# Attention blocks weighed three steps behind their scores instead of two, with the queues around it reordered

## The reference

```
s = einsum('bqhmd,bkhmd->bhmqk', q, k2) * 64 ** -0.5
s = where(dist >= 0, s + bias, NEG_INF)
p = softmax(s, axis=-1)
a = p[:, :, 0] - lam * p[:, :, 1]
o = einsum('bhqk,bkhd->bqhd', a, v)
o = rmsnorm(o, subln_gain, 1e-5) * (1 - lambda_init)
```

## Time and profile before

| | |
|---|---|
| time, median of 3 runs | 1475.78 us (1474.71 to 1475.9) |
| profiled execution | 1474.49 us, its span 1472.7 us |
| PE busy | 1399.6 us (95%) |
| DVE busy | 718.0 us (49%) |
| ACT busy | 461.9 us (31%) |
| POOL busy | 179.1 us (12%) |
| chain that ended last | PE 89%, DVE 4%, issue 2%, POOL 2%, ACT 1%, DMA 1% |
| from 290 to 511 us | PE busy 193.72 of 221.00 us |

### The profile page before, as it was taken

The page is one execution under the profiler, slowest core; times in us unless marked ns, Lnnn a source line. Parts: engine busy times, 40 slices in busy tenths (PEclk is TensorE's granted clock), DMA queues, the critical chain, the costliest instruction groups (busy, mean ns, idle before and its releaser), DMA issues.

```text
span 1472.7 us, 22577 instructions
## 1 busy us (share of the span) xinstructions
PE 1399.6 (95%) x8834; PEld 1259.0 (85%) x8834; DVE 718.0 (49%) x1066; ACT 461.9 (31%) x765; POOL 179.1 (12%) x320
## 2 busy tenths in 40 slices
PE   6999999989999799999999999999999999999993
PEld 5999999957666588889898989898989898989882
DVE  5333322265666555445636363636363535454547
ACT  4421021055555634244232323232323231313131
POOL 2243000111111221120000000000000000000017
PEclk9999999999999899999999999999999999999997
DMA  7201022274563514132111101010111010101006
GB/s 238 69 30 61 29 94 71 77 219 141 157 204 127 186 57 144 65 93 72 29 57 28 57 28 57 28 57 28 57 28 57 28 57 28 57 28 57 1 29 225
DMA packets 94154, 116.33 MB, mean 79 GB/s; under 512 B 6525, under 2 KB 65318, under 8 KB 94086
## 3 DMA queue, kind: packets, MB, share of 16 engines
q1 hardware_dynamic: 92277, 112.25, 24.0%
q10 hardware_dynamic: 1760, 3.01, 0.6%
q0 software_dynamic: 48, 0.13, 0.0%
HBM read 100.69 MB, written 14.69 MB: 78 GB/s over the span
## 4 chain that ended last, share of the span: by engine, by line
PE 89%; DVE 4%; issue 2%; POOL 2%; ACT 1%; DMA 1%; SPq 1%; DVEq 0%; ACTq 0%; POOLq 0%
PE PS L1978 36%; PE PS L2016 17%; PE PS L1716 16%; PE PS L1935 7%; PE PS L1776 2%; PE PS L1809 2%; PE PS L1832 2%; PE PS L1784 1%; DVE small L1348 1%; PE PS L1878 1%; POOL y_acc L1218 1%; PE PS L1704 1%; PE PS L2025 1%; DMA sub_gain<-in_subln_gain_dram 0%; PE PS L1863 0%
## 5 line engine op out<-in xcount | busy, mean ns | idle before, releaser
L1978 PE MATMUL PS<-act_hi,wu_hi 128*128 128x364 f32 x1056 | 347.8, 329 | 3.6 <-DVE wu_lo L1529 2.6
L1978 PE MATMUL PS<-act_lo,wu_hi 128*128 128x364 f32 x1056 | 347.6, 329 | 0.0
L1978 PE MATMUL PS<-act_hi,wu_lo 128*128 128x364 f32 x1056 | 347.4, 329 | 0.0
L1582 DVE TENSOR_TENSOR y_acc<-y_acc,PS 128x512 f32<-128x512 f32 (+1 forms) x198 | 134.9, 684 | 139.8 <-PE PS L2016 138.0
L1978 PEld LDWEIGHTS PS<-act_hi,wu_hi 128*128 128x128 f32 x1056 | 199.1, 189 | 4.3 <-DVE wu_lo L1529 2.7
L1978 PEld LDWEIGHTS PS<-act_lo,wu_hi 128*128 128x128 f32 x1056 | 199.1, 189 | 0.4
L1978 PEld LDWEIGHTS PS<-act_hi,wu_lo 128*128 128x128 f32 x1056 | 199.1, 189 | 0.0
L2016 PE MATMUL PS<-wd_hi,g_hi 128*128 128x512 f32 x360 | 143.7, 399 | 0.0
L2016 PE MATMUL PS<-wd_hi,g_lo 128*128 128x512 f32 x360 | 142.3, 395 | 0.0
L2016 PE MATMUL PS<-wd_lo,g_hi 128*128 128x512 f32 x360 | 142.1, 395 | 0.0
L1093 ACT CAST g_hi<-conv 128x1088 fp32r<-128x1088 f32 x22 | 24.3, 1103 | 275.3 <-PE PS L2016 219.3
(11 more groups left out here) (240 smaller groups left out, 2357.7 us busy)
## 6 DMA issues: line engine op xcount, KB each, us to landing
wu_raw<-in_w_up_dram SPq DMA_DIRECT2D x44, 512.0 KB, 3.9
kpage<-in_cache_k_dram SPq DMA_DIRECT2D x64, 256.0 KB, 2.9
vpage<-in_cache_v_dram SPq DMA_DIRECT2D x64, 256.0 KB, 3.0
wd_raw<-in_w_down_dram SPq DMA_DIRECT2D x22, 512.0 KB, 5.3
w_raw<-in_w_in_dram SPq DMA_DIRECT2D x20, 512.0 KB, 4.7
x_in<-in_x_prompt_dram SPq DMA_DIRECT2D x8, 512.0 KB, 6.4
wo_raw<-in_w_out_dram SPq DMA_DIRECT2D x8, 512.0 KB, 5.3
x_res<-in_x_prompt_dram SPq DMA_DIRECT2D x8, 512.0 KB, 4.1
```

Source lines behind the costliest of these rows:

```text
L1582: nc.vector.tensor_tensor(dst, dst, PS[0:r, bank, :], ALU.add).then_inc(ybank_free, 1)
L1978: mm = nc.tensor.matmul(PS[:, 3 * half + c, 0:CW], a[:, half, k, :], b[:, k, CHUNKS[c]], start=(j == 0), stop=(j == len(parts) - 1))
```

## The change

PE now weighs step i-3 in step i, directly behind `scores(i)` and ahead of the turned outputs and keys; the last three steps are weighed behind the loop. ACT does `out_square(i-3)` between the two exponents instead of at the start of the step. DVE takes the odd key page behind both maxima where the step has five or more blocks. For five blocks the scores start at column 128 (`score_from`), so that the cut between two banks falls where the bias begins. The splits of the last steps, the last sample softmax, the last squares and norms are put in a new order on ACT and DVE.

```diff
@@ -446,9 +446,13 @@
     def turns_before(i):
         return sum(turns(j) for j in range(i))
 
+    def score_from(i):
+
+        return P if width(i) == 5 else 0
+
     def score_cols(i, m):
 
-        return PS[:, 2 * m:2 * m + 2, :].rearrange("p a b -> p (a b)")[:, 0:P * width(i)]
+        return PS[:, 2 * m:2 * m + 2, :].rearrange("p a b -> p (a b)")[:, score_from(i):score_from(i) + P * width(i)]
 
     def out_bank(i):
         return 6 if i < NSTEP - 1 else 2
@@ -973,24 +977,23 @@
         act.wait_ge(dve_took, n_dve)
         for i in range(2):
             act.wait_ge(krow_stored[i], 16 * ((STEPS + 1 - i) // 2))
-        for i in range(NSTEP + 2):
-            if i >= 3:
-                out_square(i - 3)
-            if i < NSTEP and i % OB == 3 and i >= 7:
+        for i in range(NSTEP):
+            if i % OB == 3 and i >= 7:
                 take_out((i - 7) // OB)
             for n in keys_of(i):
                 if n % 2 == 0:
                     take_keys(n)
-            if i < NSTEP:
-                exponent(i, 0)
-                exponent(i, 1)
+            exponent(i, 0)
+            if i >= 3:
+                out_square(i - 3)
+            exponent(i, 1)
             if i == 2:
                 own_exponent()
             if i in SMP_STEP:
                 smp_take(SMP_STEP.index(i))
-            if 1 <= i <= NSTEP:
+            if i >= 1:
                 take_turned(i - 1)
-            if i < NSTEP and i % 4 == 3:
+            if i % 4 == 3 and i < NSTEP - 1:
                 smp_exponent(i // 8, i // 4 % 2)
                 if i % 8 == 7:
                     part_exponent(i // 8)
@@ -998,19 +1001,22 @@
                 split_w_out(3)
             if i == 30:
                 split_w_out(2)
-            if i == 31:
-                split_w_out(5)
-            if i == NSTEP:
-                split_ahead(0, slice(4, KD))
-                split_w_out(4)
-                split_ahead(0, slice(0, 4))
-                split_place(0, slice(4, KD))
+        split_ahead(0, slice(4, KD))
+        split_w_out(5)
+        take_turned(NSTEP - 1)
+        split_place(0, slice(4, KD))
+        split_ahead(0, slice(0, 4))
+        smp_exponent(NB // 2 - 1, 1)
+        part_exponent(NB // 2 - 1)
+        out_square(NSTEP - 3)
+        split_w_out(4)
+        split_place(0, slice(0, 4))
         split_w_out(1)
-        split_place(0, slice(0, 4))
+        out_square(NSTEP - 2)
         split_w_out(6)
         split_w_out(7)
+        out_square(NSTEP - 1)
         split_w_out(0)
-        out_square(NSTEP - 1)
         smp_take(NB // 2 - 1)
         split_ahead(1)
         take_out(NSTEP // OB - 1)
@@ -1465,19 +1471,18 @@
             nc.vector.tensor_tensor(wo_lo[k][:], wo_raw[k][:], wo_hi[:, k, :].bitcast(F32), ALU.subtract).then_inc(wo_lo_ready, 1)
 
         dve.wait_ge(lam_ready, 1)
-        for i in range(NSTEP + 2):
-            if 1 <= i <= NSTEP:
+        for i in range(NSTEP):
+            if i >= 1:
                 mix(i - 1)
             if i in ZERO_STEP and i >= 28:
                 zero_values()
-            if i < NSTEP:
-                row_max(i, 0)
+            row_max(i, 0)
             odd_keys = [n for n in keys_of(i) if n % 2 == 1]
-            for n in odd_keys[:1]:
-                take_keys(n)
-            if i < NSTEP:
-                row_max(i, 1)
-            for n in odd_keys[1:]:
+            if width(i) <= 4:
+                for n in odd_keys[:1]:
+                    take_keys(n)
+            row_max(i, 1)
+            for n in odd_keys[1 if width(i) <= 4 else 0:]:
                 take_keys(n)
             if i >= 3:
                 out_norm(i - 3)
@@ -1489,28 +1494,32 @@
                 nc.vector.tensor_scalar(gain_col, gain_col, 1.0 - LAM_INIT, None, ALU.mult).then_inc(rowcoef_step, 1)
             if i == 2:
                 own_softmax()
-            if i < NSTEP and i % 4 == 3:
+            if i % 4 == 3 and i < NSTEP - 1:
                 smp_softmax(i // 8, i // 4 % 2)
-            if i % 8 == 0 and 8 <= i < NSTEP:
+            if i % 8 == 0 and i >= 8:
                 smp_factors(i // 8 - 1)
             if i in ZERO_STEP and i < 28:
                 zero_values()
             if i - 1 in SMP_STEP:
                 take_rows(SMP_STEP.index(i - 1))
-            if i == 29:
+            if i == 30:
                 split_w_out(3)
-            if i == 30:
-                split_w_out(2)
-            if i == 31:
-                split_w_out(5)
-            if i == NSTEP:
-                split_rest(0, slice(4, KD))
-                split_w_out(4)
-                split_rest(0, slice(0, 4))
-                smp_factors(NB // 2 - 1)
-        for k in (1, 6, 7, 0):
-            split_w_out(k)
+        mix(NSTEP - 1)
+        zero_values()
+        split_w_out(2)
+        split_rest(0, slice(4, KD))
+        smp_softmax(NB // 2 - 1, 1)
+        split_w_out(5)
+        out_norm(NSTEP - 3)
+        split_rest(0, slice(0, 4))
+        split_w_out(4)
+        smp_factors(NB // 2 - 1)
+        split_w_out(1)
+        out_norm(NSTEP - 2)
+        split_w_out(6)
+        split_w_out(7)
         out_norm(NSTEP - 1)
+        split_w_out(0)
         split_rest(1)
         split_rest(2)
         take_rows(NB // 2 - 1)
@@ -1768,15 +1777,15 @@
                 pe.wait_ge(sat_taken, 2 * (i // QB))
                 pe.wait_ge(orows_ready, i // QB)
             qs = slice(NS + P * (n - 1), NS + P * n)
-            for c in range(0, w, 512):
-                e = min(c + 512, w)
+            edge = 512 - score_from(i)
+            parts = [(0, min(edge, w))] + [(edge, w)] * (w > edge)
+            for c, e in parts:
                 biased = max(c, b0)
                 for m in range(2):
                     d = slice(DH * m, DH * m + DH)
                     nc.tensor.matmul(score_cols(i, m)[:, c:e], qT[d, h, qs], kT[d, h, NS + c:NS + e], start=True, stop=biased >= e)
             for m in range(2):
-                for c in range(0, w, 512):
-                    e = min(c + 512, w)
+                for c, e in parts:
                     biased = max(c, b0)
                     if biased < e:
                         t = slice(biased - (w - 2 * P), e - (w - 2 * P))
@@ -1883,10 +1892,11 @@
                                       start=False, stop=True)
             mm.then_inc(pv_ready, 1)
 
-        for i in range(NSTEP + 2):
-            if i < NSTEP:
-                scores(i)
-            if i < NSTEP and i % OB == 3 and i >= 7:
+        for i in range(NSTEP):
+            scores(i)
+            if i >= 3:
+                weigh(i - 3)
+            if i % OB == 3 and i >= 7:
                 turn_out((i - 7) // OB)
             for n in keys_of(i):
                 turn_key(n)
@@ -1898,14 +1908,15 @@
                 pe.wait_ge(v_kept, 2)
                 own_scores()
                 smp_scores(0)
-            if 1 <= i < NSTEP:
+            if i >= 1:
                 smp_scores(i)
-            if 1 <= i <= NSTEP:
                 turn(i - 1)
-            if i >= 2:
-                weigh(i - 2)
             if i in SMP_STEP:
                 smp_weigh(2 * SMP_STEP.index(i))
+        weigh(NSTEP - 3)
+        turn(NSTEP - 1)
+        weigh(NSTEP - 2)
+        weigh(NSTEP - 1)
 
         def turn_rows(g):
             pe.wait_ge(oscaled_ready, g + 1)
```

## The result

The changed kernel takes 1479.5 us (median of 20 runs, 1473.69 to 1480.61) beside 1475.23 us (20 runs, 1472.07 to 1476.22) of the kernel before: a ratio of 1.002, interval 1.001 to 1.0029. The forecast was 1480.0 in a range of 1474.5 to 1484.0, so time and sign are right. Two later series of the same kernel gave 1478.9 (10 runs, ratio 1.002, 1.0008 to 1.0033) and 1479.85 us (6 runs, 1.0032, 1.002 to 1.0044). Two further executions of the kernel before, of 1749.61 and 3479.18 us, are left out everywhere.

The account below looks back on a forecast made before the run. PE, 95% busy, was taken as the bound; -1.5 + 0.45 + 3.2 + 0.3 - 0.4 - 0.1 + 2.6 = +4.5, taken as +4.2, gave 1478.7 profiled and 1480.0 us as median, range 1474.5 to 1484.0.

Parts of the forecast that it names:

- wide steps, three heads: Steps of 5 to 8 blocks: new cycle of 5.54, 6.20, 6.84 and 7.97 us, -0.5 us a head, -1.5 in three.
- steps 8 to 10 and 16 to 18: They weigh 21 blocks instead of 16, 1.2 us, plus 0.4 for a new wait; +1.6, twice: +3.2 us.
- steps 24 to 27: Last head, by the wide-step formula with 6, 7, 8, 8 blocks weighed: 30.1 against 29.77 us, +0.3.
- step 28: weigh(25) delays smp_turn, but weigh(26) is gone ahead of smp_weigh; -0.4 us taken, bounds -0.9 and +0.5.
- end, to the first product: Last step: weigh(30) waits for a later out_norm(29); first output product at 14.1 against 11.53 us, +2.6.
- rival (c): Clock: PE regains it earlier after the end's idle time, 1477.5, chance 0.08; or wide steps drop to 1.2 GHz, 1483.5, 0.10.
- the hop: Wide-step cycle: the hand-over to PE after the second exponent, between 0.04 and 0.2 us, taken as 0.16.
- a late mix: After an 8-block step, DVE's mix ends 3.5 us into the 1-block step, delaying exponents and smp_weigh: +0.4 us, twice.
- (a): At the end POOL is held by DVE's split_w_out(5): 1.2 us later, 1481.2 us, chance 0.10.
- (b): The end costs nothing, since DVE and ACT reach out_norm(29) early: 1477.4 us, chance 0.12.
- (d): Faster: in wide steps the first exponent isn't held by the key copy; 12 us over four heads, 1468, chance 0.10.
- W: Weighing's term in the wide-step cycle, between scores and key turns on PE: 0.235 us a block.

Follow-up runs that it names:

- lag2_both: Kernel before, lag two, with the odd key copy behind both maxima in wide steps and five-block scores cut at 384 columns: 1469.48 us, ratio 0.9963.
- after_again: The changed kernel run once more, unaltered, in a later series: 1478.90 us, ratio 1.0020 to the kernel before.
- keys_first: Changed kernel with key turns and turned outputs directly behind the scores on PE and weigh(i-3) behind them: 1465.49 us, ratio 0.9939 to the kernel before.
- copy_between: Changed kernel with the odd key page copied between the two maxima in every step, as before: 1487.65 us, ratio 1.0079 to the kernel before.

## Why the prediction was right, point by point

| step of the forecast | forecast | measured |
|---|---|---|
| wide steps, three heads | -1.5 | -2.2 |
| 4-block steps | +0.45 | +0.2 |
| steps 8 to 10 and 16 to 18 | +3.2 | +2.4 |
| steps 24 to 27 | +0.3 | -0.1 |
| step 28 | -0.4 | -0.35, partly at the low clock in both; +0.8 at full clock |
| steps 29 and 30 | -0.1 | -0.2 |
| end, to the first product | +2.6 | +2.1 |
| sum | +4.5, taken as 4.2 | +1.8; +2.9 with step 28 at full clock |
| clock | 0 (two rivals) | +1.3 in the mean |

**The number was right in part by luck.** The forecast of the order was +4.2. Time x clock puts the order at +1.8, and so do the steps of the two profiled executions. On that alone the time would have been 1477 us, inside the range but 3 us under the forecast. The rest of the 4.3 us between the medians is the clock, which the forecast held constant: 1.3 us in the mean, and 1.1 because the median falls into the upper group. The step that failed is the one that passes from the sum to the time: it took everything behind the first product as unchanged, and the granted clock with it. In the rivals a lower clock stood with 0.10, in wide steps. It didn't come there, since PEclk is 1.00 in all windows from 366 to 413 and from 446 to 475 us. As far as one profiled execution of the upper group shows, it came around step 28, at the start of the FFN and at its end.

**Step 28.** The forecast had -0.4 for it and the profiles give -0.35, but this agreement is false. The step ran partly at half the clock in both, and in three executions of the changed kernel it took 12.55, 12.08 and 13.95 us. The window of step 28 in lag2_both, where it does what it does in the kernel before, and then in after_again, both without low clock:

```profile
467.49:478.78 11.29, 9.73 (x132) 7.58 (x132) 3.74 (x8) 4.60 (x15) 1.85 (x6) 1.00 0.01 1
```

```profile
474.34:486.42 12.08, 9.76 (x133) 7.74 (x133) 5.62 (x13) 4.84 (x15) 1.20 (x5) 1.00 0.01 1
```

With the same work of PE the step is 0.8 us longer. In after_again PE waits 1.30 us for ACT's s_own ahead of the samples' weighing, and in lag2_both 0.35 for o_nrm. So the term had the wrong sign, and with step 28 taken at full clock the steps add up to +2.9.

**Behind the first product** some of this came back, which is why time x clock says less than 2.9. From the start of the first of the 42 output products to the end of the last it is 12.40 us before, and 11.51, 12.02 and 10.86 us in three executions of the changed kernel: more of the low stretch at this place falls into the longer wait, and less onto products. That is the first half of rival (c), which stood at 0.08: it came true in part, with 0.4 to 1.5 us.

**Wide steps.** The mechanism held to the letter: weighing with no wait, the exponent 1.12 us behind the keys (380.86 to 381.98), PE idle on the exponent. The lengths were forecast at 5.54, 6.20, 6.84 and 7.97 us and are 5.49, 6.14, 6.79 and 7.93: 0.04 to 0.06 too much each, about the size of the doubt about the hop (0.04 to 0.2, taken as 0.16).

**Where the blocks went.** The five blocks moved into steps 16 to 18 cost 1.19 us, against 5 x 0.235 = 1.18. The further +0.4 for a late mix wasn't there: PE is busy for 20.98 of 20.98 us. It was a mis-sized term, twice 0.4. In the last head the same formula gave 7.72, 7.55, 7.37 and 7.43, and 7.66, 7.45, 7.26 and 7.31 were measured.

**The end.** The wait for o_nrm was foretold at some 5 us and is 5.68, with the product 13.59 us behind the scores in place of 14.1. The half microsecond is in DVE and ACT, which reached out_square(29) at 10.16 instead of 10.5 us into the step.

**The rivals.** (a) didn't happen: DVE's split ended at 510.62 and POOL began at 510.75, and took 0.19 and 0.55 us. It was missed by 0.13 us. That POOL is held by a split shows 6 us later in the same kernel, in the timeline of POOL:

```profile
517.12 1.13 POOL L1169 TENSOR_SCALAR small<-small 128x1 f32<-128x1 f32 x1 [0.43 <-ACT PS L907]
518.34 1.41 POOL L1171 TENSOR_TENSOR small<-small 128x1 f32<-128x1 f32 x1
```

Two operations that take 0.19 and 0.55 us elsewhere take 1.13 and 1.41 here, beside DVE's splits of w_out. By the Trainium skill (SBUF — State Buffer, Who interferes with whom) a DVE instruction with two SBUF inputs contends with a GpSimd instruction that reads SBUF; the trace agrees. (b) is out by the 13.59 us. (d) is out, and keys_first shows why it was worth having: a gain of its size (12 us) was there, 13.4 measured against the changed kernel, only not through the exponent's place in ACT's queue but through that of the turns in PE's. Its mechanism, an exponent that isn't held by the key copy, did not hold: the distance from keys to exponent is 1.12 us in the changed kernel and 1.11 in keys_first. I had read in the code that the exponent is held by the key copy, and had put W into the cycle; I never asked what the kernel would do with W elsewhere, because I costed the change and not its parts.

**What the parts are worth**, in time x clock: the copy's place -5.6 (on the kernel before) or -7.0 (taken out of the changed one), the cut -2.0 or -2.5, the lag with the turns first -3.7, and weighing moved ahead of the turns +11.2 (1453.3 against 1442.1). They add up within 2 us. The change holds three gains and one loss that eats them.

## What to carry to other kernels

When a longer lag moves work away from its wait, it must not be put ahead of what feeds another engine's queue. Write the cycle as a sum with a term for each product on it, as here scores, weighing, key turn, exponents; a term that nobody on the cycle needs (weighing, 0.24 us a block) can go behind the hand-over. Here this took the whole term out of the five- to seven-block steps, and two thirds of it out of the eight-block step. Time parts of a change one by one: a change of +0.2% was made of -5.6, -2, -3.7 and +11 us.

Where a time falls into groups, compare the time multiplied by the granted clock as well as the median; it told a cut of 2 us from nothing where the medians did not. Then look where the low stretches lie, since half of each is taken off even where PE is idle. An earlier start of the products did not pay in full here: of 2.9 us on the path, 1.2 to 1.9 arrived.

An agreement of a term with a window is worth something only at the same clock: step 28 seemed 0.35 us shorter and was 0.8 longer.

## What the runs showed of the hardware

Executions of one program lie 5 us apart in two groups (1474 and 1480 us of the changed kernel), and the only difference that the records show is the granted clock, .985 against .982. Up to the end of the FFN's products the low stretches of the profiled executions are at the same few places, with the one of copy_between in step 16 as the only exception, and each begins around a wait of PE: 2.36 us for the exponent ahead of step 1 (295.94 us in the kernel before), the waits of step 28, the waits ahead of the last weighings (5.68 us in the changed kernel), 2.59 us ahead of the up products (632.32) and 3.10 us at the end of the FFN (1424.05). The longest, some 20 us at the end of the span, is in all of them too and costs nothing, as PE has no product left. What such a place costs changes from one execution to the next. The windows from 632 to 637 us of the kernels before and after show the two cases:

```profile
632.00:637.00 5.00, 4.68 (x19) 4.68 (x20) 2.85 (x4) 2.09 (x3) 0.72 (x2) 0.66 0.25 54
```

```profile
632.00:637.00 5.00, 2.62 (x16) 2.63 (x17) 4.72 (x5) 1.27 (x3) 0.00 (x0) 1.00 0.00 0
```

The wait is the same, 2.59 and 2.60 us, and ends at 632.32 and at 634.38 us; behind it the one kernel runs its up products at 1.2 GHz for a while, and the other at 2.4 at once. Output products at the two levels follow one another every 0.43 and every 0.23 us. What decides between the cases stayed open, and with it why the changed kernel meets the dearer ones more often.
